# Router product of token tile 0 inside the output projection and tile 1's shared down projection behind pair 0's up, in a two-layer MoE trunk on one Trainium2 core

## The reference

```python
x = layer_norm(ALPHA * x + h, ln1_g[i], ln1_b[i])          # h = o @ w_o
# moe_ffn
shared = (jax.nn.silu(xf @ sw1) * (xf @ sw3)) @ sw2
s = jax.nn.sigmoid(jnp.matmul(xf, router_w, preferred_element_type=jnp.float32))
sb = s + router_bias.astype(jnp.float32)
gscore = lax.top_k(sb.reshape(n_tok, N_GROUPS, N_EXPERTS // N_GROUPS), 2)[0].sum(-1)
_, gsel = lax.top_k(gscore, TOPK_GROUPS)
...
_, eidx = lax.top_k(jnp.where(emask, sb, NEG), TOP_K)
sel = jnp.take_along_axis(s, eidx, axis=-1)
gates = sel / jnp.sum(sel, axis=-1, keepdims=True) * ROUTED_SCALE
routed = grouped_experts(xf, eidx, gates, w1, w3, w2)
return (shared + routed).reshape(bsz, s_len, d)
```

## Time and profile before

| | |
|---|---|
| median of 3 runs | 1396.36 us (1395.4 to 1398.26) |
| the profiled execution's own time | 1395.3 us |
| its span in the trace | 1395.3 us |
| PE busy | 1373.6 us, 98% of the span |
| DVE, ACT, POOL busy | 36%, 24%, 7% |
| granted PE clock | full in all of the 40 slices |
| chain that ended last | PE 89%, DVE 5%, DMA 4% |
| DMA while experts stream | 420 to 422 GB/s |

### The profile page before, as it was taken

How to read it: one execution, slowest core, us unless ns; L and a number is a source line. 1 busy time by engine, 2 the same in 40 slices (tenths; PEclk the granted TensorE clock), 3 DMA queues, 4 the chain that set the end, 5 groups by cost and what they waited for, 6 DMA issues and landing times.

```text
span 1395.3 us, 21105 instructions
## 1 busy us (share of the span) xinstructions
PE 1373.6 (98%) x8662; PEld 843.4 (60%) x8662; DVE 504.6 (36%) x805; ACT 339.5 (24%) x869; POOL 98.6 (7%) x105
## 2 busy tenths in 40 slices
PE   9999999999999999999999999999999999999998
PEld 4555766566566566655497557656656666666543
DVE  1584633332323323324501146232323323233354
ACT  1243232222222222222210222222222222222212
POOL 2442210000000000000100123000000000000000
PEclk9999999999999999999999999999999999999999
DMA  9720459999999999999655404799999999999981
GB/s 301 290 92 1 181 229 420 422 420 421 421 420 421 421 421 421 420 420 386 214 198 181 182 0 182 297 422 421 421 421 421 420 422 421 420 421 421 420 348 60
DMA packets 78230, 461.85 MB, mean 331 GB/s; under 512 B 6337, under 2 KB 6561, under 8 KB 27969
## 3 DMA queue, kind: packets, MB, share of 16 engines
q1 hardware_dynamic: 75552, 452.06, 79.6%
q0 software_dynamic: 2592, 8.53, 1.9%
HBM read 459.52 MB, written 1.05 MB: 330 GB/s over the span
## 4 chain that ended last, share of the span: by engine, by line
PE 89%; DVE 5%; DMA 4%; issue 1%; ACT 1%; SPq 0%; DVEq 0%
PE ps L1058 30%; PE ps L1083 16%; PE ps L1101 9%; PE ps L1021 9%; PE ps L723 4%; PE ps L1213 4%; DMA ring<-in_exp_w_dram 3%; PE ps L827 3%; PE ps L911 3%; PE ps L935 2%; PE ps L604 1%; PE ps L1068 1%; PE ps L896 1%; PE ps L743 1%; PE ps L654 1%
## 5 line engine op out<-in xcount | busy, mean ns | idle before, releaser
L1083 PE MATMUL ps<-ring,qkT 128*64 128x512 f32 x1024 | 233.9, 599 | 0.4 <-DMA ring<-in_exp_w_dram 0.4
L1058 PE MATMUL ps<-ring,proj 128*64 128x256 f32 x2048 | 227.0, 379 | 1.8 <-DMA ring<-in_exp_w_dram 1.8
L1058 PEld LDWEIGHTS ps<-ring,proj 128*64 128x64 f32 x2048 | 146.7, 137 | 89.1 <-issue 17.1
L1869 DVE TENSOR_TENSOR o_tok<-ps,o_tok 128x1024 f32<-128x1024 f32 x124 | 151.7, 1224 | 91.0 <-PE ps L1101 90.0
L1875 DVE TENSOR_TENSOR y_lo<-ps,y_hi 128x1024 fp32r<-128x1024 f32 x62 | 75.9, 1224 | 226.7 <-ACT y_hi L1428 226.7
L1861 DVE SCALAR_TENSOR_TENSOR roped<-roped,rows,ps 128x256 f32<-128x256 f32 x64 | 30.7, 480 | 306.9 <-ACT roped L1401 298.9
L1083 PEld LDWEIGHTS ps<-ring,qkT 128*64 128x64 f32 x1024 | 67.8, 136 | 112.4 <-issue 110.0
L1058 PE MATMUL ps<-ring,pT 128*64 128x256 f32 x1024 | 121.5, 379 | 0.0
L1058 PE MATMUL ps<-ring,gb_row 128*64 128x256 f32 x1024 | 121.4, 379 | 0.0
L1428 ACT ACTIVATE y_hi<-ps 128x1024 fp32r<-128x1024 f32 x62 | 63.5, 1023 | 216.0 <-PE ps L1083 216.0
L1101 PE MATMUL ps<-y_hi,selT 128*128 128x512 f32 x248 | 109.3, 441 | 0.0
(11 more groups left out here) (275 smaller groups left out, 1466.6 us busy)
## 6 DMA issues: line engine op xcount, KB each, us to landing
ring<-in_exp_w_dram SPq DMA_DIRECT2D x180, 2048.0 KB, 15.1
ring<-in_exp_w_dram SPq DMA_DIRECT2D x24, 1024.0 KB, 7.1
ring<-in_od_w_in_dram SPq DMA_DIRECT2D x6, 2048.0 KB, 8.7
ring<-in_ple_w_gate_dram SPq DMA_DIRECT2D x4, 2048.0 KB, 13.2
ring<-in_ev_w_in_dram SPq DMA_DIRECT2D x3, 2048.0 KB, 20.0
ring<-in_sh_w_dram SPq DMA_DIRECT2D x6, 1024.0 KB, 7.8
ring<-in_ev_w_o_dram SPq DMA_DIRECT2D x2, 2048.0 KB, 10.2
ring<-in_od_w_o_dram SPq DMA_DIRECT2D x2, 2048.0 KB, 8.5
```

Of the source, the lines that this page charges most:

```text
L1058: ins = pe.matmul(ps[b * SLOTS:(b + 1) * SLOTS, 2, w * FE:(w + 1) * FE], xe(odd, c)[:, u * P + b * SLOTS:u * P + (b + 1) * SLOTS], views[b ...
L1083: ins = pe.matmul(ps[b * SLOTS:(b + 1) * SLOTS, 4 + half, :], hT[:, f, b * SLOTS:(b + 1) * SLOTS], views[b][:, f, half * PIECE:(half + 1) ...
L1869: dve.tensor_tensor(y_acc[:, t, :], ps[:, bank:bank + 2, :].rearrange("p b n -> p (b n)"), y_acc[:, t, :], ALU.add)\
```

## The change

In the changed program PE does three chunks of `wo(L, 1, 1)`, the router product of tile 0, then the other five chunks. DVE chooses tile 0's experts (`choose(L, 0)`, the old instructions as a function) after the statistics of the first half of tile 1's sum and before its second half. The shared up projection of tile 0 runs three groups before tile 1's transposes and one behind them. The `place` products come ahead of the shared down projection of tile 0. Tile 1's down projection goes into banks 6 and 7 behind pair 0's `exp_up`. SP loads w1 and w3 of expert 3 after the shared up projection and not after the shared down projection; ACT issues the load of its w2, after it has copied tile 1's shared result.

```diff
+                    if k == shared_item[L] + RING:
+                        sp.wait_ge(sem("shared_up"), NT * (L + 1))
+                        up_load(k % RING, a["exp_w1"][L, k - e0], a["exp_w3"][L, k - e0])
+                        k += 1
+                        continue
...
                 transpose_tile(x_tok, 0)
-                wo(L, 1, 1, range(DC))
+                wo(L, 1, 1, range(0, 3))
+                pe.wait_ge(sem("layer_loaded"), 48 * (L + 1))
+                router(L, 0)
+                wo(L, 1, 1, range(3, DC))
...
-                up_tile(ks % RING, 0, between).then_inc(sem("shared_up"), 1)
-                wait_tile("xT", 3 * L + 1, 1)
-                router(1)
-                up_tile(ks % RING, 1, None).then_inc(sem("shared_up"), 1)
-
+                up_tile(ks % RING, 0, 2, second_tile).then_inc(sem("shared_up"), 1)
+                router(L, 1)
+                up_tile(ks % RING, 1).then_inc(sem("shared_up"), 1)
+                places()
                 pe.wait_ge(sem("shared_h"), NT * L + 1)
                 down_all(ks % RING, [0]).then_inc(sem("shared_down"), 1)
-
-                pe.wait_ge(sem("router_dve"), NT * (L + 1))
...
-                ins.then_inc(sem("place_mm"), 1)
-                pe.wait_ge(sem("shared_h"), NT * L + 2)
-                down_all(ks % RING, [1]).then_inc(sem("shared_down"), 1)
...
                     exp_up(m, o, odd, u, par, first and M0 == 0)
+                    if first:
+                        pe.wait_ge(sem("shared_h"), NT * (L + 1))
+                        down_all(ks % RING, [1], bank=4).then_inc(sem("shared_down"), 1)
+                    if isinstance(m, int) and m == 1:
+                        pe.wait_ge(sem("shared_added"), NT * (L + 1))
...
                 rsqrt_guess()
                 copy_T("xT_act", tp, 0)
+                router_exp(0)
                 rsqrt_guess()
-                for t in range(NT):
...
+                copy_T("xT_act", tp, 1)
+                router_exp(1)
+                shared_silu(0)
                 shared_silu(1)
                 tp += NT
...
+                shared_add(0, 0)
...
-                for u in range(4):
+                silu(0)
+                shared_add(1, 6)
+                slot = (shared_item[L] + RING) % RING
+                act.dma_start(ring[:, slot, DOWN0:DOWN0 + 2 * D], a["exp_w2"][L, RING - 1].rearrange("(p c) f -> p (c f)", c=2))\
+                   .then_inc(down_loaded[slot], 16)
+                act_step(0, 0, True, 0, silu_done=True)
...
                         xs = summed[:, t, half * PIECE:(half + 1) * PIECE]
+                        if which == 1 and t == 1 and half == 1:
+                            choose(L, 0)
...
-                dve.wait_ge(sem("layer_loaded"), 48 * (L + 1))
+                choose(L, 1)
                 for t in range(NT):
```

133 lines of the change are left out of this document (67 added, 66 removed).

## The result

| | before | after |
|---|---|---|
| median | 1396.36 us (5 runs, 1395.4 to 1398.26) | 1403.0 us (5 runs, 1401.84 to 1404.08) |
| ratio after / before, 95% interval | | 1.0045, 1.0034 to 1.0055 |
| profiled execution: its own time, its span | 1397.14, 1395.3 | 1401.84, 1399.7 |
| PE busy | 1373.6 us | 1374.0 us |

The change costs 6.6 us, 0.45%: slower than the 0.2% that can be told from no change, and above the end of the range, 1400.6. One entry of the table ahead of the prediction was wrong: it gave 1395.3 us as the own time of the profiled execution of before, which is its span; the time was 1397.14. So that execution was 0.8 us slower than the median and not 1.1 faster. Since I applied a difference to the median, the forecast doesn't move by this.

A forecast was written before the change was run, and what follows sets the result against it. PE, busy 98%, was taken to bound the kernel, with the DMA stream later by 0.9 us at phase ends. PE's +1.9 a layer, less absorbed waits, left 1.0 and 0.6: +1.6, 1398.0 us, range 1394.8 to 1400.6.

The forecast's parts named there:

- Step 1: Tile 0's router and choice ahead of tile 1's norm: PE waits about 1.8 us before transposes, cost 1.3 us a layer.
- Step 2: At the places after tile 1's up: PE no longer waits for the choice of experts, gain 0.7 us a layer.
- Step 3: Between places and first gather: cover gone, POOL's casts hold DVE's chain to `sel`, cost 1.3 us a layer.
- the first is held to 179.0: In DVE's chain behind the places: the subtraction waits only until 179.0, halfway through POOL's casts (177.1 to 180.9).
- Step 4: Tile 1's down behind pair 0's `exp_up`: PE's sum unchanged, term zero, between -0.1 and +0.3 us.
- Step 5: Expert weight stream: ends as before, so waits of 0.9 us (layer 0) and 1.3 (layer 1) absorb PE's lateness.
- I take a stream that ends as before: End of the expert phase: weight loads land when they did before, within -0.5 and +0.5 us.
- the absorption: At the last pair: PE's 1.9 us lateness shrinks by old weight waits to 1.0 (layer 0) and 0.6 (layer 1).
- The third rival: Expert phase: expert 3's w2 and pair 2's late w2 make the stream 1.9 us late; 1400.1 us, chance 0.18.
- the norm's wait between 1.5 and 2: Before tile 1's transposes: PE waits for the norm 1.5 to 2 us in each layer, before 0.35.
- a new wait before the gather: Before the first gather: PE newly waits 1 to 1.3 us for DVE's `sel`.
- if PE still waits for weights by 0.9, the third holds: End of the expert phases: a remaining 0.9 us weight wait would mean a late stream; forecast gone or under 0.2.

The follow-up runs named there:

- one-chunk kernel: The changed kernel with tile 0's router product behind the first chunk of `wo` instead of the third; median 1401.15 us, ratio 1.0032 to before.
- router-only kernel: The kernel before with the early router, choice and places alone, tile 1's down and expert 3's loads left as before; 1396.94 us, ratio 1.0003.
- no-subtraction kernel: The changed kernel without subtracting one from the places, the comparison table and thresholds raised by one instead; 1399.22 us, ratio 1.0018 to before.
- down-only kernel: The kernel before with tile 1's down behind pair 0's up, expert 3's earlier loads and ACT's part alone; 1406.45 us, ratio 1.0068.
- The filled wait: The changed kernel with four products of constants on PE ahead of the first gather; 1402.09 us, ratio 1.0045 to before.

## Why the prediction was wrong

**Step 1 was right.** `choose` took 5.5 us (152.46 to 157.97), the norm's second half was taken up at 158.00, PE waited 1.66 (forecast 1.8, and 1.5 to 2 as its sign). The one-chunk kernel removes it and the router-only kernel has it alone, at +0.55 with step 2. **Step 2 was right**: no wait at the places.

**Step 3 had the mechanism and a wrong size**: 1.3 forecast, 1.88 measured. The term that failed is "the first is held to 179.0", the end of the first cast. The earlier trace rows didn't speak against it: the `tensor_tensor` began in the first cast and was held to its end, and the `tensor_scalar` was held to the second's end but had also begun in the second (178.15). The subtraction, a `tensor_scalar` that began inside the first cast, was held through both, 2.82 us, and so were all 18 such subtractions in the nine executions where one begins there. The reduction and the masking, 0.5 us together, then came behind the casts instead of during them, and `sel` was ready 0.6 us later. The no-subtraction kernel shows the same from the other side. The rule of the Trainium skill ("SBUF — State Buffer", section "Who interferes with whom", its single rule) holds in its core: in the no-subtraction kernel the reduction, with one input, ran in 0.29 during the first cast, and in both kernels every instruction of a contending kind that met a cast was blocked until a cast had ended. That a blocked instruction may also miss the turn between two casts I didn't reckon with, and it is the 0.5.

**Step 4 was right in its own terms and wrong in its scope.** ACT's copy and DMA issue (0.39 us) held nothing up. But the eight matmuls weren't moved to a neutral place: they left the one where they covered DVE's way from the places to `sel`, and went between pair 0's and pair 1's gates.

**Step 5 failed in layer 0**, at the sentence "I take a stream that ends as before". I reasoned from pair 0's gate, which is earlier, and from slack in the stream. The end follows pair 1's gate. So with PE 2.43 late at pair 1 the stream was 2.43 + 0.31 late, PE's wait for weights stayed and grew by 0.3 (0.9 to 1.2), and nothing was absorbed: +2.74 where the step had +1.0. In layer 1 the absorption did come: PE was 4.05 late there (2.43 and the clock's 1.6), 1.3 of waits for weights went, which makes 2.75, and 2.65 was measured. But that was luck: the stream ended 439.28 behind pair 1's gate, 0.9 sooner than before's 440.19. In the second execution of the same kernel, 4.07 late at that gate, it ended at 440.45, PE waited 1.19 for weights, and the layer is +3.84. The third rival came nearest to this outcome, at 1400.1 and 0.18, with a reason of its own (the w2's volume and pair 2's late w2) that three runs refuted. Its mechanism is a race I had seen and put in the wrong place.

**What was missing** is the granted clock. In six profiled executions with a wait of 1.9 us before the first gather, 7 of 12 layers lost their clock behind it; with the 2.6 us of the down-only kernel 2 of 2 did; in six executions where that wait was 0.9 or less, or filled, 0 of 12. Each loss costs about 1.6 us on PE. The filled wait, with nothing else changed, kept the clock in both layers; that is two layers, against 5 of 12 that kept it by themselves, so that the wait brings the loss rests on all the executions together and not on this one. I had priced each wait by its length alone. In this stretch of before the longest idle of PE was 0.55 and the clock stayed full. But the profile of before did show the loss elsewhere, behind the 1.69 us wait of layer 0's attention, and the page's digits hid it. A long wait isn't the only occasion either: at 701 to 706 us the clock fell in seven of thirteen executions with no idle over 0.38 just ahead.

**The sum.** Forecast +1.6. Measured by the parts: layer 0 +2.74, layer 1 +2.65, outside the span +0.3, which is 5.7, and 1.3 more in an execution that loses its clock in layer 0 too (+4.02 there). The medians say +6.6 and +7.1. Between 1.6 and 5.7 stand step 3's size, 2 x 0.5; the absorption that failed in layer 0, 0.9 + 0.3; the clock in layer 1, 1.6; and the 0.3 outside the span. The absorption in layer 1 is in this sum only because that execution's stream was short. The rest up to the medians, 0.9 to 1.4, stays open: the clock in layer 0 (+1.3 in the second execution), the stream's scatter in layer 1 (1.2 between the two) and the low stretch between the layers (1.64, in the second execution and not in the first) can each make it, and two profiled executions can't tell their shares in a median. The terms are read in single executions and aren't exact to better than a few tenths.

**What held of the signs**: the norm's wait between 1.5 and 2, no wait at the places, a new wait before the gather (but 1.9 and not 1 to 1.3), "if PE still waits for weights by 0.9, the third holds": it did, in layer 0.

## What to carry to other kernels

An instruction group that seems only to be moved may be the cover of a chain on other engines; list what ran beside it before it goes, and price the bare chain. Where a transfer stream is released by the consumer's own gates, find the gate to which its end is tied, by measuring from a gate to the end in both traces: lateness ahead of that gate isn't absorbed by the wait at the end. And add to any new PE wait of 2 us the chance that the clock drops behind it. Whether it has dropped behind waits already is read from windows of a few microseconds; a digit of the page covers too much.

## What the runs showed of the hardware

- The granted clock can fall behind a single wait of 1.9 us in an engine otherwise 98% busy, in 7 of 12 cases here, and then a gather matmul of 512 columns comes every 0.43 us instead of 0.23. Behind a wait of 1.7 us in attention, where PE was busy for 1.0 to 1.2 of each 2 us, it fell in 11 of 13. It also fell in 7 of 13 executions at 701 to 706 us with no idle over 0.38 in the 14 us before.
- A DVE `tensor_scalar` that began 1.0 us into the first of two back-to-back POOL casts was held 2.82 us, to the end of the second, and so in all 18 layers with such an instruction; a two-input instruction in the same place (`scalar_tensor_tensor`, the no-subtraction kernel) was held 0.72, to the end of the first. Why the two differ isn't settled.
- A 2 MB load that shared the DMA engines with a 1 MB load from ACT's queue took 12.7 us, where the same load with only 16 KB from ACT beside it took 11.1.
- The nine kernels that issue a DMA from ACT have 2.1 us outside their span, the three that don't 1.8, in every run. The nine also share the moved down projection, so the cause isn't shown.
- The full stream shows short pauses: in layer 0 of the changed kernel three landings came 1.6 us late, at 247.2, 392.9 and 538.6, 145.7 apart; before's layer 1 has them at 1058.0 and 1203.6. Such pairs or triples about 145.7 apart are in nearly every layer, sometimes split over two landings, not in step with the program, and their cause stays open. How they fall may be the scatter of the 440 us.
